# Stick-breaking attention: short and long query rows alternate, narrower value matmuls, values of a group in one piece

## The reference

```python
z = einsum('bqhd,bkhd->bhqk', q, k) * 64 ** -0.5
mask = k_pos[None, :] < q_pos[:, None]
log_keep = where(mask, log_sigmoid(-z), 0.0)
suffix = cumsum(log_keep, axis=3, reverse=True) - log_keep
a = where(mask, exp(log_sigmoid(z) + suffix), 0.0)
out = einsum('bhqk,bkhd->bqhd', a, v)
```

## Time and profile before

| What | Value |
|---|---|
| median of three runs | 3030.11 us |
| profiled execution, its own time | 3031.01 us |
| its span | 3028.9 us |
| busy in the span: PE, DVE, ACT, POOL | 2880.8, 1164.9, 949.5, 620.0 us |
| stick-breaking stage | from 1799 to 2107 us of the span |
| in 1840 to 1880 us busy: PE, ACT, DVE, POOL | 38.55, 31.37, 27.71, 21.61 of 40 us |

### The profile page before, as it was taken

The page is one execution under the profiler, slowest core; times in us unless marked ns, Lnnn a source line. Parts: engine busy times, 40 slices in busy tenths (PEclk is TensorE's granted clock), DMA queues, the critical chain, the costliest instruction groups (busy, mean ns, idle before and its releaser), DMA issues. The chain is left out here.

```text
span 3028.9 us, 41450 instructions
## 1 busy us (share of the span) xinstructions
PE 2880.8 (95%) x15811; PEld 2504.7 (83%) x15811; DVE 1164.9 (38%) x1782; ACT 949.5 (31%) x1924; POOL 620.0 (20%) x478
## 2 busy tenths in 40 slices
PE   7979997799999999999899989997999999999998
PEld 6868886689998999889798875554898899889987
DVE  5656653343332333223311017776442333223324
ACT  4334443322211122113222228886231122112212
POOL 3100000112211121112121215555121121112211
PEclk9989998899999999999899999999999999999999
DMA  4311103501110111101235356552210111101111
GB/s 138 88 47 42 42 28 94 181 8 56 56 42 28 42 55 48 33 29 42 82 124 166 122 150 153 142 137 91 77 50 28 42 55 48 35 28 55 48 35 77
DMA packets 188027, 215.48 MB, mean 71 GB/s; under 512 B 17281, under 2 KB 148865, under 8 KB 187905
## 3 DMA queue, kind: packets, MB, share of 16 engines
q1 hardware_dynamic: 187904, 213.82, 23.4%
HBM read 166.17 MB, written 47.61 MB: 71 GB/s over the span
## 5 line engine op out<-in xcount | busy, mean ns | idle before, releaser
L1476 DVE TENSOR_TENSOR x<-m_ps,x 128x512 f32<-128x512 f32 x324 | 223.8, 691 | 606.0 <-PE m_ps L76 606.0
L1512 DVE TENSOR_TENSOR m_sq<-m_relu 128x384 f32<-128x384 f32 x192 | 170.8, 889 | 505.0 <-ACT m_relu L1408 505.0
L74 PE MATMUL m_ps<-h_h,m_up0h 128*128 128x384 f32 x768 | 257.1, 335 | 0.0
L76 PE MATMUL m_ps<-h_h,m_up0l 128*128 128x384 f32 x768 | 256.7, 334 | 0.0
L75 PE MATMUL m_ps<-h_l,m_up0h 128*128 128x384 f32 x768 | 256.7, 334 | 0.0
L74 PE MATMUL m_ps<-h_h,m_up1h 128*128 128x384 f32 x768 | 256.5, 334 | 0.0
L75 PE MATMUL m_ps<-h_l,m_up1h 128*128 128x384 f32 x768 | 256.5, 334 | 0.0
L76 PE MATMUL m_ps<-h_h,m_up1l 128*128 128x384 f32 x768 | 256.5, 334 | 0.0
L1408 ACT ACTIVATE m_relu<-m_ps 128x384 f32<-128x384 f32 x192 | 94.5, 492 | 507.6 <-PE m_ps L76 507.6
L1403 ACT CAST m_dn0h<-m_dn_raw 128x1024 fp32r<-128x1024 f32 x16 | 16.8, 1051 | 547.1 <-PE m_ps L76 547.0
L2295 POOL TENSOR_TENSOR e_b<-e_b,e_r 128x128 f32<-128x128 f32 (+7 forms) x128 | 155.3, 1216 | 129.3 <-DVE e_r L2348 129.3
(11 more groups left out here) (494 smaller groups left out, 7173.4 us busy)
## 6 DMA issues: line engine op xcount, KB each, us to landing
m_up_raw<-in_mlp_w_up SPq DMA_DIRECT2D x64, 512.0 KB, 4.6
m_dn_raw<-in_mlp_w_down SPq DMA_DIRECT2D x64, 512.0 KB, 3.4
h_raw<-scratch_oT SPq DMA_DIRECT2D x4, 1536.0 KB, 15.1
scratch_qr<-a_qrst SPq DMA_DIRECT2D x9, 512.0 KB, 3.4
a_x<-in_x_prompt SPq DMA_DIRECT2D x8, 512.0 KB, 4.9
b_qr<-scratch_qr SPq DMA_DIRECT2D x4, 1024.0 KB, 6.7
scratch_oT<-b_o SPq DMA_DIRECT2D x32, 128.0 KB, 1.7
new_p_sb_k<-d_rows SPq DMA_DIRECT2D x16, 256.0 KB, 2.1
```

The costliest lines, as they stand in the source:

```text
L74: pe.matmul(out, w[0], m[0], start=start, stop=False)
L76: return pe.matmul(out, w[1], m[0], start=False, stop=stop)
L1476: dve.tensor_tensor(x[:, t, cols], bank[:, 4 + n % 3, :], x[:, t, cols], ALU.add).then_inc(added.sem, 1)
L1512: dve.tensor_tensor(sq[n % 2][:], relu[n % 2][:], relu[n % 2][:], ALU.mult).then_inc(sq_done.sem, 1)
```

## The change

Rows now alternate in length. With `short` = 0 to 3, a group has the query blocks `short` and 7 - `short` of both heads, so a pair runs q = 0,7,0,7, 1,6,1,6, 2,5,2,5, 3,4,3,4, and every group has nine blocks a head. `pt` is indexed by key block alone and needs no zeros. For key blocks up to `short` the value matmul takes all 256 columns, for the others the 128 of the long row. All values of a group are issued in one piece, in the first step behind the group. The output is stored as two pieces of 128 columns.

```diff
     def where(n):
         m = n % SbSchedule.PAIR_STEPS
-        return n // SbSchedule.PAIR_STEPS % 2, m // 2 % 2, 2 * (m // 4) + m % 2
+        short = m // 4
+        return n // SbSchedule.PAIR_STEPS % 2, m // 2 % 2, NPT - 1 - short if m % 2 else short
+
+    @staticmethod
+    def turns(n):
+
+        q = SbSchedule.where(n)[2]
+        return [range(k, min(k + 4, q + 1)) for k in range(0, q + 1, 4)]
...
             def store(i, g):
                 o_done.wait(sp, S.GROUPS * i + g + 1)
-                cols = slice((g % 4) * GQ, (g % 4 + 1) * GQ)
-                sp.dma_start(scratch["oT"][2 * i + g // 4, :, cols], o_st[g % 4][:]).then_inc(
+                short, tall = g % 4, NPT - 1 - g % 4
+                rows = scratch["oT"][2 * i + g // 4, :, 0:SEQ].rearrange("p (q c) -> p q c", c=P)
+                sp.dma_start(rows[:, short:tall + 1:tall - short], o_st[g % 4][:]).then_inc(
                     o_out[g % 4].sem, 16)
...
-                    if j == 0 and values_of is not None and values_of % 4 == 3:
+                    if j == 0 and values_of is not None and values_of % 4 == 1:
                         output(i, values_of // 4)
...
-            for x in pt:
-                dve.memset(x[:, 0, 0:P], 0.0).then_inc(const_done.sem, 1)
...
-            def values(i, g, quarter):
-
-                pair, last_q = g // (S.GROUPS // 2), 2 * (g % 4) + 1
-                order = [(last_q, 0)] + [(k, k + 1) for k in range(last_q)]
-                if quarter == 0:
-                    for u in range(2):
-                        t_out[u].wait(pe, TURNS[u] * i + copies(S.before(4 * g + 4), u))
-                    if g % (S.GROUPS // 2) == 0:
-                        v_in[pair].wait(pe, 16 * (i + 1))
-                    o_done.wait(pe, S.GROUPS * i + g)
-                for k, slot in order[len(order) * quarter // 4:len(order) * (quarter + 1) // 4]:
+            def values(i, g):
+
+                pair, short = g // (S.GROUPS // 2), g % 4
+                for u in range(2):
+                    t_out[u].wait(pe, TURNS[u] * i + copies(S.before(4 * g + 4), u))
+                if g % (S.GROUPS // 2) == 0:
+                    v_in[pair].wait(pe, 16 * (i + 1))
+                o_done.wait(pe, S.GROUPS * i + g)
+                for k in range(NPT - short):
+                    cols = slice(0 if k <= short else P, GQ)
                     for a in range(2):
                         rows = slice(a * SB_DIM, (a + 1) * SB_DIM)
-                        done = pe.matmul(bank[rows, 7, 0:GQ], v[pair][:, k, rows], pt[2 * (g % 2) + a][:, slot, :],
-                                         start=k == last_q, stop=k == last_q - 1)
-                if quarter == 3:
-                    done.then_inc(pv_done.sem, 1)
+                        done = pe.matmul(bank[rows, 7, cols], v[pair][:, k, rows], pt[2 * (g % 2) + a][:, k, cols],
+                                         start=k == 0, stop=k == NPT - 1 - short)
+                done.then_inc(pv_done.sem, 1)
...
-                    if j == 0 and values_of is not None:
-                        values(i, values_of // 4, values_of % 4)
+                    if j == 0 and values_of is not None and values_of % 4 == 0:
+                        values(i, values_of // 4)
```

More of the change, by code:

```diff
@@ L1916, in turned_by @@
         body, step = divmod(n, cls.STEPS)
-        return cls.before(cls.STEPS) * body + cls.before(step) + len(transpose_tasks(cls.where(step)[2]))
+        return cls.before(cls.STEPS) * body + cls.before(step) + len(cls.turns(step))
     @classmethod
@@ L1936, in tasks @@
         sample = cls.sample_task(n)
-        return [("prompt", t) for t in transpose_tasks(cls.where(n)[2])] + ([sample] if sample else [])
+        return [("prompt", t) for t in cls.turns(n)] + ([sample] if sample else [])
     @classmethod
@@ L1996, in sb_attention_stage @@
         rest = [sb(f"e_r{u}", [P, SEQ + 1]) for u in range(2)]
-        o_st = [sb(f"e_o{u}", [P, GQ]) for u in range(4)]
+        o_st = [sb(f"e_o{u}", [P, 2, P]) for u in range(4)]
         zero = sb("e_zero", [P, 1])
@@ L2086, in turned_rows @@
         def turned_rows(n, task):
-            s0, at = task[0][1], (n % 2) * P
-            return pt[n // 2 % 4][:, s0:s0 + len(task), at:at + P]
+            at = (n % 2) * P
+            return pt[n // 2 % 4][:, task[0]:task[0] + len(task), at:at + P]
         def turned_in(m, task):
@@ L2240, in output @@
                 o_out[g % 4].wait(act, 16 * (S.GROUPS // 4 * i + g // 4))
-                act.copy(o_st[g % 4][:], bank[:, 7, 0:GQ]).then_inc(o_done.sem, 1)
+                act.copy(o_st[g % 4][:], bank[:, 7, 0:GQ].rearrange(
+                    "p (s c) -> p s c", s=2)).then_inc(o_done.sem, 1)
             def step(i, n, last, values_of=None):
@@ L2329, in _ @@
             dve.memset(zero[:], 0.0).then_inc(const_done.sem, 1)
-            const_done.wait(dve, 8)
+            const_done.wait(dve, 4)
             def transposed(i, n):
@@ L2467, in turn @@
                 weighted.wait(pe, S.STEPS * i + n + 1)
-                for c, (k, _) in enumerate(task):
+                for c, k in enumerate(task):
                     t = pe.transpose(task_bank(m)[:, c * P:(c + 1) * P], take(n)[:, k * P:(k + 1) * P], ident[:])
                 t.then_inc(t_done.sem, 1)
-            def values(i, g, quarter):
-                pair, last_q = g // (S.GROUPS // 2), 2 * (g % 4) + 1
-                order = [(last_q, 0)] + [(k, k + 1) for k in range(last_q)]
-                if quarter == 0:
-                    for u in range(2):
-                        t_out[u].wait(pe, TURNS[u] * i + copies(S.before(4 * g + 4), u))
-                    if g % (S.GROUPS // 2) == 0:
-                        v_in[pair].wait(pe, 16 * (i + 1))
-                    o_done.wait(pe, S.GROUPS * i + g)
-                for k, slot in order[len(order) * quarter // 4:len(order) * (quarter + 1) // 4]:
+            def values(i, g):
[7 more added lines that the diff above has]
+                    cols = slice(0 if k <= short else P, GQ)
                     for a in range(2):
                         rows = slice(a * SB_DIM, (a + 1) * SB_DIM)
-                        done = pe.matmul(bank[rows, 7, 0:GQ], v[pair][:, k, rows], pt[2 * (g % 2) + a][:, slot, :],
-                                         start=k == last_q, stop=k == last_q - 1)
-                if quarter == 3:
-                    done.then_inc(pv_done.sem, 1)
+                        done = pe.matmul(bank[rows, 7, cols], v[pair][:, k, rows], pt[2 * (g % 2) + a][:, k, cols],
+                                         start=k == 0, stop=k == NPT - 1 - short)
+                done.then_inc(pv_done.sem, 1)
             def step(i, n, last, values_of=None):
@@ L2501, in body @@
                     step(i, n + S.VALUES_LAG, last, n)
-            const_done.wait(pe, 8)
+            const_done.wait(pe, 4)
             for n in range(S.AHEAD):
```

## The result

The changed kernel takes 3078.45 us (median of four runs, 3076.3 to 3080.67). Its ratio to the kernel before is 1.0160, with a 95% interval of 1.0148 to 1.0173: 48 us slower, where 27 us (3057) had been forecast, with a range of 3024 to 3092. The span of the profiled execution went from 3028.9 to 3074.2 us, +45.3.

The account below looks back on a forecast made before the run. PE bounds the kernel now; a loop through all four engines was to set the period afterwards. 3031.0 + 7.3 (start) + 23.4 (seven periods) - 4.0 (end) = 3057.7 profiled, 3057 us as median, range 3024 to 3092.

Parts of the forecast that it names:

- The loop: Between groups' values: scores, sigmoids, scan, POOL, scan and DVE's copy run in series, 41.0 us a pair against 37.6.
- both sides: Scan waits for POOL through the shared buffer; values wait for DVE's last copy and hold up the next scores.
- POOL's wait: A group's second long-row scan waits until POOL has weighed the first, 1.36 to 2.00 us, through one `rest` buffer.
- What TensorE saves: Value matmuls on PE: from 12.3 to 8.5 us a pair, 3.8 less, 30 us in all.
- Narrow values at half price: Value matmuls of 128 columns: 0.205 us a block, half of the 0.41 for 256 columns.
- A run's fixed cost: Each run of value matmuls on PE: 0.29 us beside its blocks, with 4 runs a pair instead of 14.
- a fall in the waits: Rival "The clock falls": PE idles 1.0 to 3.2 us ahead of each group's values; slower still, within a shared 0.25.
- dearer: Case that the loop costs more than summed, through narrow values (3083 us) or the clock: chance 0.25.
- the row: Profile row at 1826 to 1831 with 1.3 us idle, weighed for the clock rival as most new waits are under 3.
- The start: Start of the stage: long rows 1, 3, 5, 7 pass through one buffer, first values at 1818.8 instead of 1811.54, +7.3.
- The end: End of the stage: nothing is scanned in the last group, 25.6 us from the last pair's first values against 29.6, -4.0.
- POOL's wait is covered: Rival: DVE's work between long rows hides POOL, 4 us less a pair, period 37, about 3030 us; chance 0.11.

Follow-up runs that it names:

- quarters: Changed kernel with the values cut into four quarters in four steps, and three rest buffers: 3011.8 us, ratio 0.9948; with one rest buffer for long rows 3027.9 us.
- the fastest kernel: Changed kernel with values one step later and three rest buffers (with three output buffers): 2997.5 us, ratio 0.9903.

## Why the prediction was right, and where it was off

**The direction and the mechanism held.** The loop was forecast as 10.82, 9.91, 9.01 and 11.24 us, and the turns of the trace without a fall of the clock are 10.89, 9.95, 9.10 and 11.25. The kernel with junk matmuls, whose clock stays full, takes 3059.9 us; the sum said 3057, with 41.0 us a pair for 41.2. That the loop needs both sides is shown by the runs: taking POOL's wait away, or moving the values one step, brings 52 and 48 us, each about the whole loss with the clock's part in it, and both together bring 81.

**What TensorE saves is confirmed only in part.** 30 us were summed, and the kernel without either wait is 31 us faster than before, but that the two agree is in part luck. Narrow values at half price are shown (2.12 us for one wide and seven narrow blocks). A run's fixed cost came out at 0.15 to 0.20 us between quarters and one piece, where 0.29 had been taken; with 0.20 the sum gives an estimated 23 us. The old order with late values, which by the sum saves as much, gained 10 us, with 10 us more of PE's named waits than before (25.3 against 14.8). So the work saved is nearer 20 us there and 28 us in the fastest kernel; why the two differ is left open.

**The term that was mis-sized is the clock.** The sum had the clock at its full level throughout, and a fall in the waits stood beside it as a rival, inside "dearer" with a chance of 0.25, priced at 24 us for one fall a pair. Falls are what happened, and they cost 18.5 us by the run with junk matmuls: twelve in eight pairs, at some 1.5 us each where 2.9 had been put on one. Falls came oftener than once a pair and cost less than summed, which nearly cancels, so it is luck in part that the rival's 3081 lies close to the 3078.5 measured. The step that failed is the sentence "I give the row more weight, as most of the new waits are under 3 us". The row at 1826 to 1831 had 1.3 us of idle time; but the loop's own waits had been put at up to 3.2 us, and two a pair were 2.6 to 2.7; to those the other row, 2.5 us idle and then a clock of 0.53, was the nearer one. By the Trainium skill ("TensorE: Matmul & The Clock Gate", the section on HAM oscillation) bursts of matmuls divided by waits are throttled anew in every turn. The trace agrees in part: the clock is at 0.88 and 0.91 in two windows of 40 us and at 1.00 in a third, with twelve falls in some thirty turns, and the waits here, 2.7 us at most, are shorter than those of the example in that section.

**Smaller points.** The start was put at +7.3 us and was +3.9, with junk matmuls 1818.93 - 1811.54 = +7.4. Why the start came out so differently in the two is not shown. The end was put at -4.0 and was -0.9; 2.3 us of the difference lie in the last pair's first turn, 12.20 us (2121.26 to 2133.46) where 9.91 had been summed, with a granted clock of 0.66 and 0.50 behind its start. DVE's wait for POOL was to go over 30 us and was 27.4. Values' waits were to be 50 to 70 us and were 55.5, but under the name of ACT's copy, whose end lies 0.5 us ahead of DVE's.

**The price of the rival "POOL's wait is covered" was near.** The time without that wait was worked out as about 3030; the run with three rest and three output buffers gave 3026.3. The wait went there by another buffer, not by DVE's own work.

## What to carry to other kernels

When work is gathered into one piece on the engine that is the bound, ask what stands behind it in its queue and who waits for that: here the piece waited for a copy and held the scores that the copy's successor needed, and one step's delay of the piece was worth 48 us. When the order of rows changes, look which of them share a buffer: `n % 2` with alternating lengths put all long rows into one. And where waits of 2 to 3 us on TensorE come back every 10 us, look for the clock behind them besides the waits themselves: here its falls were 18.5 us of a loss of 48.

## What the runs showed of the hardware

Junk matmuls made a kernel 18.5 us faster, since they kept TensorE's clock at 2.4 GHz. There are 27 a pair, 0.24 us each by the row of eleven (22 instructions) in 2.62 us: 52 us of added work in eight pairs. The length of a wait alone did not decide on a fall. The wait of 2.74 us ahead of the values at 1847.29 left the clock at 1.00, the equally long one ahead of 1931.96 did not. Of two waits of 1.77 us ahead of a second group's values, the one at 1911.61 left the clock full, and the one at 1999.67 did not. Windows around that one (busy times and clock):

```profile
1997.00:1999.60 2.60, 0.90 (x7) 0.39 (x5) 2.07 (x5) 2.60 (x7) 2.60 (x4) 0.99 0.00 0
1999.60:2003.00 3.40, 3.33 (x24) 2.71 (x26) 2.27 (x2) 0.78 (x2) 2.71 (x5) 0.51 0.02 5
```

What decides was not tried.
